# Norm factor applied as projection tiles leave their banks, x turned block by block between first products

## The reference, cut to what matters

```
hn   = x * rsqrt(mean(x*x, -1) + eps) * pre_norm_g      # x: (512, 2048)
proj = hn @ w_in                                        # w_in: (2048, 7832)
q, kv6, gates, z_a, feat_b, z_b = split(proj)
mix  = concat(nsa(q, kv6, gates) * silu(z_a), rwkv7(feat_b) * silu(z_b))
x    = x + rms_norm(mix @ w_out, post_norm_g)
```

## Time and profile before

| what | us |
|---|---|
| median of three runs | 3189.02 |
| lowest and highest | 3187.07, 3192.75 |
| the profiled execution's own time | 3188.98 |
| its span | 3187.2 |
| PE busy in the span | 3144.7 |
| DVE busy | 1769.4 |
| ACT busy | 1254.5 |

### The profile page before, as it was taken

How to read it: one execution, slowest core, us unless ns; L and a number is a source line. 1 busy time by engine, 2 the same in 40 slices (tenths; PEclk the granted TensorE clock), 3 DMA queues, 4 the chain that set the end, 5 groups by cost and what they waited for, 6 DMA issues and landing times. The chain is left out here.

```text
span 3187.2 us, 51639 instructions
## 1 busy us (share of the span) xinstructions
PE 3144.7 (99%) x21539; PEld 2570.3 (81%) x21539; DVE 1769.4 (56%) x3074; ACT 1254.5 (39%) x1992; POOL 185.4 (6%) x148
## 2 busy tenths in 40 slices
PE   8999999999999999999999999999999999999999
PEld 6877777777778778678888888888888888888787
DVE  5235555565666653644457775335556655665822
ACT  4124343433444422423346665333344434443421
POOL 0000000001010101000001010110000000000000
PEclk9999999999999999999999999999999999999999
DMA  8433333333232443333331213533223323332452
GB/s 247 115 77 93 90 93 96 97 90 87 62 96 70 151 140 94 115 95 103 102 103 53 60 50 119 152 111 110 87 83 96 93 74 99 93 93 80 159 159 79
DMA packets 492526, 324.25 MB, mean 102 GB/s; under 512 B 27130, under 2 KB 448605, under 8 KB 491782
## 3 DMA queue, kind: packets, MB, share of 16 engines
q1 hardware_dynamic: 492294, 320.94, 34.7%
HBM read 276.05 MB, written 44.85 MB: 101 GB/s over the span
## 5 line engine op out<-in xcount | busy, mean ns | idle before, releaser
L535 PE MATMUL PS<-XH,WHT 128*128 128x512 f32 (+1 forms) x2224 | 899.9, 405 | 2.9 <-DVE AR L1032 1.2
L523 DVE TENSOR_TENSOR WLT<-AR,WHT 128x1024 fp32r<-128x1024 f32 (+1 forms) x430 | 526.5, 1230 | 657.3 <-ACT WHT L517 656.8
L537 PE MATMUL PS<-XH,WLT 128*128 128x512 f32 (+1 forms) x2224 | 872.5, 392 | 0.0
L517 ACT ACTIVATE WHT<-AR 128x1024 fp32r<-128x1024 f32 (+1 forms) x430 | 446.9, 1042 | 632.6 <-PE PS L537 473.4
L536 PE MATMUL PS<-XL,WHT 128*128 128x512 f32 (+1 forms) x1712 | 670.1, 391 | 0.0
L535 PEld LDWEIGHTS PS<-XH,WHT 128*128 128x128 f32 (+1 forms) x2224 | 416.7, 187 | 105.3 <-issue 11.3
L537 PEld LDWEIGHTS PS<-XH,WLT 128*128 128x128 f32 (+1 forms) x2224 | 416.9, 187 | 98.1
L536 PE MATMUL PS<-ARR,WHT 128*128 128x512 f32 x1024 | 404.4, 395 | 0.0
L536 PEld LDWEIGHTS PS<-XL,WHT 128*128 128x128 f32 (+1 forms) x1712 | 320.9, 187 | 71.8 <-issue 4.8
L536 PEld LDWEIGHTS PS<-ARR,WHT 128*128 128x128 f32 x1024 | 192.4, 188 | 40.1 <-issue 0.2
L535 PE MATMUL PS<-XL,WHT 128*128 128x512 f32 x512 | 203.4, 397 | 0.1
(11 more groups left out here) (492 smaller groups left out, 5126.8 us busy)
## 6 DMA issues: line engine op xcount, KB each, us to landing
AR<-b_w_in SPq DMA_DIRECT2D x128, 512.0 KB, 4.0
AR<-w_in SPq DMA_DIRECT2D x122, 512.0 KB, 4.1
AR<-a_w_in SPq DMA_DIRECT2D x48, 512.0 KB, 4.3
AR<-w_out SPq DMA_DIRECT2D x32, 512.0 KB, 4.4
AR<-a_w_out SPq DMA_DIRECT2D x32, 512.0 KB, 4.0
AR<-b_w_out SPq DMA_DIRECT2D x32, 512.0 KB, 4.0
proj_scratch<-AR SPq DMA_DIRECT2D x33, 256.0 KB, 2.3
AR<-a_w_kv_up SPq DMA_DIRECT2D x32, 256.0 KB, 4.0
```

Source lines behind the costliest of these rows:

```text
L517: self.nc.scalar.activation(self.shaped(self.high, n), self.shaped(self.raw, n), ACT.Copy).then_inc(self.s_high, 1)
L523: self.nc.vector.tensor_tensor(self.shaped(self.low, n), self.shaped(self.raw, n), f32(self.shaped(self.high, n)), ALU.subtract).then_inc( ...
L535: mm(out, wh, xh[k0 + c], start=(start and c == 0), stop=False)
L537: last = mm(out, wl, xh[k0 + c], start=False, stop=(stop and c == nk - 1))
```

## The change

The norm factor leaves `start`'s path. x comes in four column quarters (all tokens, 4 blocks of features each), with unit 0 ahead of the first and unit 1 ahead of the second; the gain rows come by a DMA that ACT issues. PE turns one feature block of 512 tokens at a time (`turn`), the first four ahead and each further one inside `ready`, three blocks ahead of the products. ACT rounds bank times gain to `XH`, DVE makes `XL` from the bank in one instruction (`to_low`), ACT copies even blocks and DVE odd blocks to `RES`. The Squares come between blocks 9 and 15, the diagonals after, and the factor is spread and copied to `layer1_factor` behind both pairs. The residual copy is cut in four stores, each with one weight load behind it, and whoever waited for `res_out` now waits for four. In `nsa` and `rwkv` each evacuation multiplies by the factor; a gate tile is first scaled, then ACT takes the sigmoid of the scaled copy, and DVE multiplies both (`gated`) in a later place of its queue. In `rwkv` the store of a gate tile and its sigmoid are placed later as well. `pair` waits for each unit by itself.

```diff
+def layer1_factor(k):
+
+    return k.EXT[:, 0, :]
+
...
             split = k.cc["bones"][0]
+
+            def columns(g):
+                sp.dma_start(X[:, :, g * NCOL:(g + 1) * NCOL], d["x"][0, :, g * NCOL:(g + 1) * NCOL].rearrange("(b p) n -> p b n", p=P)).then_inc(x_in[g], 16)
+
+            def part(n):
+                r, b, cc, src = parts[n]
+                m, w = src.shape
+                sp.dma_start(rows[r:r + m, b, cc:cc + w], src).then_inc(r_in, 16)
             sp.dma_start(k.C[:, 0:split], d["consts"][:, 0:split]).then_inc(small, 16)
-            for b in range(TB):
-                sp.dma_start(X[:, b, :], d["x"][0, b * P:(b + 1) * P, :]).then_inc(x_in[b], 16)
+            st.load(sp, 0)
+            columns(0)
+            st.load(sp, 1)
+            columns(1)
+            columns(2)
+            st.load(sp, 2)
+            st.load(sp, 3)
+            columns(3)
             sp.wait_ge(zeroed, 1)
-            for n, (r, b, cc, src) in enumerate(parts):
-                m, w = src.shape
-                sp.dma_start(rows[r:r + m, b, cc:cc + w], src).then_inc(r_in if n else g_in, 16)
-                if n == 0:
-                    for u in range(4):
-                        st.load(sp, u)
+            for n in range(1, len(parts)):
+                part(n)
             sp.dma_start(k.C[:, split:], d["consts"][:, split:]).then_inc(c_in, 16)
-            sp.wait_ge(d_copied, len(by_dve))
-            sp.wait_ge(a_copied, len(by_act))
-            sp.dma_start(k.RESD.rearrange("c p t -> p c t"), k.RES[:, :, :]).then_inc(res_out, 16)
-            for u in range(4, 8):
-                st.load(sp, u)
+            for g in range(TB):
+                copied(sp, 4 * g + 2)
+                copied(sp, 4 * g + 3)
+                sp.dma_start(k.RESD[4 * g:4 * g + 4, :, :].rearrange("c p t -> p c t"), k.RES[:, 4 * g:4 * g + 4, :]).then_inc(res_out, 16)
+                st.load(sp, 4 + g)
...
+            def turn(c):
+                if c % 4 == 0:
+                    pe.wait_ge(x_in[c // 4], 16)
+                if c >= 4:
+                    copied(pe, c - 4)
+                for b in range(TB):
+                    last = nc.tensor.transpose(TURN[c % 4][:, b * P:(b + 1) * P], X[:, b, c * P:(c + 1) * P], C("ident"))
+                last.then_inc(turned, 1)
+
+            def ready(c):
+                if c and c + 3 < KT:
+                    turn(c + 3)
+                pe.wait_ge(low, c + 1)
             pe.wait_ge(small, 16)
-            for b in range(TB):
-                pe.wait_ge(x_in[b], 16)
-                for g in range(4):
-                    if b:
-                        copied(pe, b - 1, g)
-                    for c in range(4):
-                        last = nc.tensor.transpose(TURN[g][:, c * P:(c + 1) * P], X[:, b, (4 * g + c) * P:(4 * g + c + 1) * P], C("ident"))
-                    last.then_inc(turned, 1)
             pe.wait_ge(g_in, 16)
-            nc.tensor.transpose(ROWB[:, 0:NG1], rows[0:NG1, 0, :], C("ident")[0:NG1, 0:NG1]).then_inc(g_t, 1)
+            nc.tensor.transpose(ROWB[:, 0:NG1], gain[0:NG1, :], C("ident")[0:NG1, 0:NG1]).then_inc(g_t, 1)
+            for c in range(4):
+                turn(c)
+            st.pair(pe, (0, 1), PAIR, k.XHT, k.XLT, 0, True, False, ready)
+            st.pair(pe, (2, 3), PAIR, k.XHT, k.XLT, 8, False, True, ready)
             for b in range(TB):
                 pe.wait_ge(diag, b + 1)
                 nc.tensor.matmul(RSB[:, b * P:(b + 1) * P], C("ones"), DG[:, b, :], start=True, stop=True).then_inc(spread, 1)
-
-            def ready(c):
-                pe.wait_ge(low_v, c + 1)
-            st.pair(pe, (0, 1), PAIR, k.XHT, k.XLT, 0, True, False, ready)
             pe.wait_ge(r_in, 16 * (len(parts) - 1))
+            copied(pe, KT - 4)
             for b in range(2):
                 last = nc.tensor.transpose(TURN[0][:, b * P:(b + 1) * P], rows[:, b, :], C("ident"))
             last.then_inc(r_t, 1)
-            st.pair(pe, (2, 3), PAIR, k.XHT, k.XLT, 8, False, True, ready)
             pe.wait_ge(c_in, 16)
 
         @block.scalar
...
-            def copy(n):
-                b, g = by_act[n]
-                to, frm = block_of(b, g)
-                act.wait_ge(turned, 4 * b + g + 1)
-                A(to, frm, ACT.Copy).then_inc(a_copied, 1)
-
             def to_high(c):
-                act.wait_ge(scaled, c + 1)
-                A(k.XH[:, c, :], TM[c % 4], ACT.Copy).then_inc(high, 1)
+                act.wait_ge(turned, c + 1)
+                A(k.XH[:, c, :], TURN[c % 4][:, :], ACT.Copy, scale=k.prm("pre_g", c)).then_inc(high, 1)
+
+            def copy(c):
+                act.wait_ge(low, c + 1)
+                A(k.RES[:, c, :], TURN[c % 4][:, :], ACT.Copy).then_inc(a_copied, 1)
+
+            def square(b):
+                for g in range(TB):
+                    act.wait_ge(x_in[g], 16)
+                A(JUNK, X[:, b, :], ACT.Square, accum_out=S4[:, b:b + 1]).then_inc(summed, 1)
+                act.wait_ge(summed, b + 1)
+                A(R4[:, b:b + 1], S4[:, b:b + 1], ACT.Sqrt, scale=1.0 / D, bias=EPSC).then_inc(rooted, 1)
+            nc.scalar.dma_start(gain[0:NG1, :], parts[0][3]).then_inc(g_in, 16)
             act.wait_ge(eps_set, 1)
             A(ROOT, EPSC, ACT.Sqrt)
-            for b in range(TB):
-                act.wait_ge(x_in[b], 16)
...
             st.split_high(act, 0)
-            to_high(0)
-            st.split_high(act, 1)
-            for c in range(1, KT):
+            act.wait_ge(g_c, 1)
+            for c in range(KT):
                 to_high(c)
-                if c in (3, 5):
-                    st.split_high(act, (c + 1) // 2)
+                if c in (0, 5, 7):
+                    st.split_high(act, 1 + (0, 5, 7).index(c))
+                if c % 2:
+                    copy(c - 1)
+                if c in (9, 11, 13, 15):
+                    square((c - 9) // 2)
             st.split_high(act, 4)
             st.split_high(act, 5)
...
-            def scale(c):
-                if c >= 4:
-                    dve.wait_ge(low_v, c - 3)
-                V.scalar_tensor_tensor(out=TM[c % 4], in0=k.RES[:, c, :], scalar=k.prm("pre_g", c), in1=RSB[:, :], op0=ALU.mult, op1=ALU.mult).then_inc(scaled, 1)
-            for n, (b, g) in enumerate(by_dve):
-                if b and g == 0:
-                    factor(b - 1)
-                to, frm = block_of(b, g)
-                dve.wait_ge(turned, 4 * b + g + 1)
-                V.tensor_copy(to, frm).then_inc(d_copied, 1)
-            factor(TB - 1)
+            def to_low(c):
+                dve.wait_ge(high, c + 1)
+                V.scalar_tensor_tensor(out=k.XL[:, c, :], in0=TURN[c % 4][:, :], scalar=k.prm("pre_g", c), in1=f32(k.XH[:, c, :]), op0=ALU.mult, op1=ALU.subtract).then_inc(low, 1)
+            dve.wait_ge(small, 16)
             dve.wait_ge(g_t, 1)
             V.tensor_copy(k.PRM[:, 0:NG1], ROWB[:, 0:NG1]).then_inc(g_c, 1)
+            st.split_low(dve, 0)
             dve.wait_ge(g_c, 1)
-            dve.wait_ge(d_copied, len(by_dve))
-            dve.wait_ge(a_copied, len(by_act))
+            for c in range(KT):
+                to_low(c)
+                if c % 2:
+                    dve.wait_ge(low, c + 1)
+                    V.tensor_copy(k.RES[:, c, :], TURN[c % 4][:, :]).then_inc(d_copied, 1)
+                if c in (0, 5, 7):
+                    st.split_low(dve, 1 + (0, 5, 7).index(c))
+                if c in (11, 13, 15):
+                    factor((c - 11) // 2)
+            factor(TB - 1)
+            st.split_low(dve, 4)
             dve.wait_ge(spread, TB)
-            for c in range(KT):
-                scale(c)
-                if c in (0, 1, 4, 6):
-                    st.split_low(dve, (0, 1, 4, 6).index(c))
-                if c:
-                    dve.wait_ge(high, c)
-                    low(V, c - 1, low_v)
-                if c == 12:
-                    dve.wait_ge(r_t, 1)
-                    V.tensor_copy(k.PRM[:, NG1:], TURN[0][:, NG1:2 * P])
-            dve.wait_ge(high, KT)
-            low(V, KT - 1, low_v)
-            st.split_low(dve, 4)
+            V.tensor_copy(layer1_factor(k), RSB[:, :])
             st.split_low(dve, 5)
+            dve.wait_ge(r_t, 1)
+            V.tensor_copy(k.PRM[:, NG1:], TURN[0][:, NG1:2 * P])
...
-        for n in units:
-            pe.wait_ge(self.s_low, n + 1)
         for c in range(nk):
             ready(k0 + c)
             for n, bank in zip(units, banks):
+                if c == 0:
+                    pe.wait_ge(self.s_low, n + 1)
                 wh, wl = self.shaped(self.high, n)[:, c, :], self.shaped(self.low, n)[:, c, :]
...
             sp.wait_ge(tab0, 1)
             sp.dma_start(TAB[0:NBUCKET, :], d["rel_bias_table"]).then_inc(tab_in, 16)
-            sp.wait_ge(res_out, 16)
+            sp.wait_ge(res_out, 16 * TB)
...
             def sigmoid(t):
                 kind, c, _ = tiles[t]
```

(118 more changed lines are left out.)

15 lines of the change are left out of this document (6 added, 9 removed).

## The result

| what | before, us | after, us |
|---|---|---|
| median (of 4 and 4) | 3190.11 | 3204.14 |
| lowest and highest | 3187.07, 3192.75 | 3203.19, 3206.65 |
| profiled execution | 3188.98 | 3204.64 |
| its span | 3187.2 | 3202.8 |

The ratio is 1.0047, 95% interval 1.0031 to 1.0063: the change made the kernel some 14 us slower (15.6 between the spans of the two profiled executions). The forecast was no change that can be measured, 3188.5 in a range that ended at 3191.5. It was wrong.

The account below looks back on a forecast made before the run. PE, busy 99%, was taken to bound the kernel, leaving some 42 us of idle and half speed time. Gains of 0.2 at the start and 0.3 from evacuations made 0.5 us: 3188.5 from 3189.02, range 3184.0 to 3191.5.

Parts of the forecast that it names:

- Step 7: Evacuations in `nsa` and `rwkv`: products with the factor replace copies; gain 0.3 us, bounds +0.6 and -1.9.
- The rival that gave 3204: In `nsa`, gates hold DVE's queue and eight heads pay 1.9 us each: 15 us slower, 3204; chance 0.07.
- Steps 1 and 2: In `start`: first x at 8.3, unit 1 ready at 12.4, pairs end at 39.0 instead of 49.1.
- Steps 3 and 4: In `start`: ACT and DVE keep up with PE, ACT within 0.2 us; DVE's tail ends at 43.2.
- Step 5: `nsa`'s start waits for the last of four residual stores, landing at 47.3 (46.5 to 48.8); PE resumes at 48.1.
- the term for the three loads in front: In SP's queue, three weight loads ahead of the last residual store delay it 5.3 us, less 0.5 for overlap.
- The count of pieces behind the 1.0: In SP's queue at the start, about 2,600 pieces held; SP through when 3,670 are done, at 14.7, 1.0 us earlier.
- Step 6: PE's clock falls in the gap before `nsa`; half speed costs 2.2 us (1.5 to 3.4), leaving a gain of 0.2.
- Step 8: Arena, semaphore per unit and gain load on ACT's queue: nothing; a load queued behind 1.5 MB would cost 0.2 us.

Follow-up runs that it names:

- experiment 2: Kernel before, with only SP's order changed: a late gate tile's store waits for DVE's level 2 of the next pair, the spill behind it; 3203.4 us, ratio 1.0045.
- experiment 1: Kernel after, with two statements exchanged so that SP issues the spill ahead of the late gate tile's store; 3184.24 us, 0.9987 of the kernel before.
- experiment 6: Experiment 4 with the four Squares and the diagonals two blocks earlier (Squares at blocks 7 to 13); 3180.87 us, 0.9978 of the kernel before.
- Experiment 4: Experiment 1 with the large constants ahead of the 26 small rows and two weight loads behind the last residual store; 3181.99 us, 0.9979 of the kernel before.
- experiment 5: Experiment 1 with the first column quarter of x loaded ahead of weight unit 0; 3184.68 us.
- Experiment 7: Experiment 4 with 16 useless products on PE in the gap before `nsa`; 3181.25 us, 0.9974 of the kernel before.
- experiment 3: Experiment 2 with the store's wait one level earlier, level 1 of the next pair; 3193.9 us, 1.0017 of the kernel before.
- experiment 8: Experiment 6 with 8 useless products in the gap before `nsa`; 3181.28 us, 0.9976 of the kernel before.

## Why the prediction was wrong

**The sum as it was and as it came.** In the spans of the two traces:

| stretch | predicted | measured |
|---|---|---|
| up to the end of `nsa` | -0.2 | -1.2 |
| `rwkv` up to the copy of pair 3 | -0.3, for all of `rwkv` | -0.7 |
| from there to the copy of pair 7 | 0 | +19.8 |
| the rest | 0 | -2.3 |
| sum | -0.5 | +15.6 |

**Step 7 failed.** It costs the moved pieces of a gate tile as work of ACT and DVE ("the moved sigmoid ... falls into a 1.91 us idle time"). It was right on that: the sigmoid at 998.32 held up nobody. The same edit moved a third thing, the store, behind a wait for `z_gated`, and the step didn't name what is queued behind this wait on SP: `spill(i - 2)` stands two lines below in the code. The chain was there to be read. SP waits for DVE's level 2; the spill's second half leaves at 1004.96 instead of 996.09; it lands at 1008.0; ACT's `out_squares` needs it; PE's `decays` needs ACT. From the trace of before it could have been priced too: the spill was issued at 996.09 and used at 1001.53, and in the next pair ACT waited 0.52 us for it, so a delay of 9 us was bound to show. The step put the loss at 1.9 us at most; 19.8 were measured where the wait stands. The prediction's own test for it, windows past 200 us that lose more than 1 us of PE each, is what the trace then showed.

**Where 19.8 us come from.** These are the stretches from the copy of pair 3 to that of pair 7, in the kernel before and in the kernel after. PE has the same work in both.

```profile
947.52:1134.90 187.38, 178.81 (x3706) 142.21 (x3705) 118.44 (x242) 81.42 (x148) 23.70 (x17) 1.00 0.33 101
945.65:1152.79 207.14, 186.92 (x3705) 147.21 (x3704) 120.67 (x247) 81.11 (x148) 23.30 (x17) 0.95 0.30 91
```

PE is without work for 8.6 us before and for 20.2 after: 11.7 more, of which 10.9 are the two waits for ACT. The same matmuls take 8.1 us longer. After each wait PE runs at half speed, as this window of the kernel after shows, 0.50 granted:

```profile
1009.00:1014.00 5.00, 4.83 (x36) 3.11 (x37) 0.00 (x0) 1.31 (x4) 0.76 (x1) 0.50 0.03 10
```

The half speed stretches that this trace has between the two copies and the one before has not are 6.8, 10.2 and 3.4 us long. The first two begin while PE still waits, so 15.4 us of them hold work, and half of that is 7.7, close to the 8.1. In experiment 2 the same reading gives 9.1 us without work and 6.8 of longer matmuls, for 15.9. So some three fifths of the loss are waits and two fifths the clock behind them. That is read from the traces; no run keeps the waits and holds the clock up.

**The rival that gave 3204** landed on the number and not on the cause. It put 15 us into `nsa`, where DVE's queue would be held by the gates. `nsa` lost nothing.

**Steps 1 and 2, first products and pairs.** x landed at 8.30 (8.3 forecast), unit 1's products began at 12.47 (12.4), the pairs ended at 39.3 (39.0). Two errors cancel in the last. The products at 11.34 to 11.89 stand 0.24 to 0.31 apart, so the clock was up already, and the 1.3 us for half speed until 15 was not paid. This is partly luck: in experiment 1, whose start is the same program, three products ran at half speed and the pairs ended at 39.9. And a turn of four transposes between products takes more than four times 0.083: at 16.92 it holds PE for 0.35, and the product behind it takes 0.32 to its successor instead of 0.23. That is 0.44 a turn, 5.3 for twelve instead of 4.0. The 16 transposes ahead took 3.04 us, not the 2.4 of 0.15 each; this cost nothing, since unit 1 came later still.

**Steps 3 and 4, ACT and DVE.** PE waited 0.18 us within the pairs, so ACT and DVE kept up, with as little to spare as was said: two blocks earlier for the Squares and PE waits 1.17 (experiment 6). DVE's tail ended at 43.3 (43.2).

**Step 5, the stores.** Right in kind: DVE's 3.00 us wait is for the DMA. The last landing was 46.3, 1.0 before the 47.3 forecast and 0.2 below the lower bound. SP was through with its loads at 15.26, 0.4 and not 1.0 us earlier than before, but the 26 rows took less time and the constants were issued at 25.33 (25.4), so the stores began 1.1 us earlier, as the sum had it. What was too dear is the term for the three loads in front, 5.3 less 0.5 for the overlap: 46.3 + 1.1 - 43.5 leaves 3.9 instead of 4.8. The count of pieces behind the 1.0 doesn't hold: by its own timetable the 3,670th piece is through at 14.9, and in the trace some 4,300 were when SP went on, so about 2,000 were outstanding and not 2,600. The last store was issued at 37.67, right behind the copy of block 15 (DVE, until 37.60), and took 8.6 us to land, so its data didn't hold it up, as was said. Experiment 4 confirms what the step is about: without the loads in between it no longer gates.

**Step 6, the clock.** Half speed followed the gap, from 45.2 for 6.8 us. PE's stream lies in it from 47.07 to 52.0; at 0.43 instead of 0.23 for a product that is 2.3 us (2.2 forecast). The stream is then where it would be had it begun at 49.4 at full speed, against 50.47: 1.1, and `nsa` ended 1.2 us earlier. How much half speed costs here varies between executions: by the same working 1.8 us in experiment 1, whose start is the same program, and 2.6 and 2.7 in experiments 4 and 5. The start of the stream plus this cost gives the end of `nsa` within 0.1 us in the kernels before and after and in experiments 1, 4, 5, 6 and 7: the last output is made 612.9 us later in each. So of the gain of 1.2 us some 0.8 hang on how long half speed happens to last: with the same start experiment 1 ends `nsa` at 661.4, the kernel after at 662.2. Experiment 7 gives 2.1 us by removing it.

**Step 7, what of it held.** An evacuation with the factor costs what the copy did; this is the group of the kernel after (lowest, median and highest ns).

```profile
L2080 DVE TENSOR_TENSOR AR<-PS,EXT x17: 679/684/693, 673.9 to 1104.3; 128x512 f32<-128x512 f32 x17
```

In `rwkv` the gain was larger than the 0.3 forecast. In experiment 1, where the spill is out of the way, its lead over the kernel before grows from 2.0 at the end of `nsa` to 3.9 at the last copy, 1.9 us. Which part gives it (the bank that no longer waits for a sigmoid is the forecast one) was not separated.

**Step 8.** The gain's rows landed 2.4 us after their issue and the cost of 0.2 wasn't paid. ACT issued them at 0.73, ahead of SP's first weight load (1.18), so this doesn't show what a load issued by ACT does once 1.5 MB are queued on SP.

## What to carry to other kernels

When an instruction with a new wait is put into an in-order queue, read the queue below it to the end of the loop body, the DMA queue of SP above all, and follow each entry to whoever waits for its landing; price the edit by the least slack among all repetitions, not by the first. A store that nobody needs soon may come late, but then it belongs behind the transfers that somebody needs: two lines exchanged turned 0.47% slower into 0.13% faster. And where a wait falls on TensorE's stream, count with the half speed after it: here the slower matmuls added 8.1 us to 11.7 us of waits.

## What the runs showed of the hardware, unexpected

**A remainder of more than one length.** From the last copy of `out_squares` to the end of the span all kernels run the same program. It took 2052.3 to 2052.9 us in before and experiments 1 and 2, 2049.7 to 2050.2 us in after and experiments 3, 4, 6, 7 and 8, and 2051.3 in experiment 5. In every trace there is one stretch at the lower clock in it. In the first group it begins 170.4 to 172.3 us behind that copy, in the second 168.5 to 169.5, and it is 10.2 us long in both; in experiment 5 it begins 173.0 us behind it and is 6.8 us long. A window of the kernel before lies in it, with PE at 2.28 us of 5:

```profile
1305.00:1310.00 5.00, 2.28 (x4) 0.62 (x4) 3.20 (x6) 1.32 (x2) 0.00 (x0) 0.53 0.02 4
```

So the place and the length of this stretch sort all ten traces. That they are what decides was not tested, and what sets them is open. It means that up to 3 us of any difference here can have nothing to do with an edit: more than experiments 4, 6, 7 and 8 differ from one another, and about a third of the 7 us by which they are faster than the kernel before.

**The clock's rise at the start.** Before, the transposes ran at the lower level from 6.54 to about 12; after, they began at 8.30 and the clock was up by 11.3, 3 us later instead of 5. The order isn't what sets this: in experiments 1, 4, 6, 7 and 8, the same program up to there, it was up 3.3 to 5.3 us after the first transpose, and in experiment 5, where PE waited 1.13 us ahead of its first product, 8.8 us.
